# Output projection behind all token groups, in seven block products for eight

## The chip, the cores and the metric

The kernel runs on one core of one Trainium2 chip. The metric is device time in microseconds (us). Three runs of the kernel before took 2799.24, 2799.42 and 2800.96 us. All data are float32, one launch, inputs and output in the chip's memory (DRAM).

## What is computed

One layer over 2048 tokens of width 2048. An input projection to 5376 columns feeds three head groups: A (16 heads of chunked sliding-window attention over 128 keys, with sinks and a bias), B/C/X (a gated convolution of three taps), M (cross-attention into 256 memory tokens). Each output is gated, all are put side by side and mapped by one output projection, w_out (2048 x 2048):

```python
h = rmsnorm(x, ln_gain[l])
proj = h @ w_in[l]
q_a, k_a, v_a, g_a, b_c, c_c, x_c, g_c, q_m, g_m = jnp.split(proj, offsets, axis=-1)
o_a = swa_sink_attention(q_a, k_a, v_a, q_norm_a[l], k_norm_a[l], sinks[l], bias)
o_c = short_gated_conv(b_c, c_c, x_c, conv_w[l])
mem_h = rmsnorm(mem, mem_ln_gain[l])
o_m = memory_cross_attention(q_m, mem_h, w_mem_kv[l], q_norm_m[l], k_norm_m[l])
mixed = jnp.concatenate([jax.nn.silu(g_a) * o_a, jax.nn.silu(g_c) * o_c,
                         jax.nn.silu(g_m) * o_m], axis=-1)
x = x + mixed @ w_out[l]
```

## The kernel before

**Work and slots.** The tokens are four groups of 512. A float32 product is made of three matmuls on a split of each operand into a part in the type float32r and the rest: hi x hi, hi x lo, lo x hi (`split_product`, lines 1146 to 1148). Weights come in slots of 512 KB: SyncE (SP) loads a slot into `raw` (four places), ScalarE (ACT) casts its two halves to `w_hi` (`high`, line 501), GpSimd (POOL) subtracts to get `w_lo` (`low`, line 431), and TensorE (PE) runs 24 matmuls of 128x512 with it. w_hi and w_lo have room for two slots, so ACT may cast the second half of slot s+2 only when PE is through with slot s.

**A group** is 84 slots of flow and 32 of output. Slots 0 to 3 are the block KV; then come blocks of 8 slots: QM (to slot 11), QA0 (19), QA1 (27), C (35), X (43), B (51), GM (59), GC (67) and the two gates of A (75, 83). Each block fills the four PSUM banks acc0 to acc3, and the next block's first matmul into a bank waits until the bank is read. X and B are read by VectorE (DVE; lines 1030 and 1037), a gate by ACT (tanh, line 590) and DVE (line 1003, then line 1010 times the attention output). In between, at slots given by tables (`SCORES_AT` and others, in slot numbers of the group), 24 attention units run: scores on PE, softmax on DVE and ACT (lines 921 to 957), a move of the turned probabilities by DMA, the split of them (`pt_hi` on ACT, `pt_lo` on DVE, line 889), values on PE, and `attention_sum` on DVE (line 901). A unit's values come three slots after its scores; units of M start every slot, those of A nearly all every second. Every engine takes its instructions in the order in which its program lists them, so the tables set that order.

**Output part.** Behind the flow of a group stand 4 x 8 slots: for each block of 512 output columns, `mixed` (split into `mix_hi`, `mix_lo`) times w_out. In the same stretch the next group's x is prepared, one tile of 128 tokens per column block: load (line 508), squares on ACT (516), mean and scale on DVE (741 to 747), a transpose in 16 DVE operations (`x_flip`, line 775), the split into `h_hi` (ACT, 543) and `h_lo` (DVE, 784). DVE then adds x to the bank (line 1131), ACT stores.

Of the kernel before, what the change touches and what calls it, by code (L numbers as in the profile page):

```python
# [105 lines left out]
X_LOAD_S, X_SQ_S, RESID_S = 0, 2, 3  # L106
X_HIGH_AT = {5: (0, 1), 6: (2, 3)}
# [14 lines left out]
def program(nc, x, mem, ln_gain, w_in, q_norm_a, k_norm_a, sinks, conv_w, mem_ln_gain, w_mem_kv,  # L122
            q_norm_m, k_norm_m, w_out, rel_bias, one_hot, bias_rows, out):
# [3 lines left out]
    with ctx:  # L127
# [6 lines left out]
        def sem(name):  # L134
            return ctx.enter_context(nc.semaphore(name))
# [35 lines left out]
        flipped = nc.alloc_sbuf_tensor_at("flipped", [P, KT, P], F32, offset=flipped_at)  # L171
# [136 lines left out]
        def q_blocks(kind):  # L308

            return slice(12, 16) if kind == 0 else slice(4 * kind - 4, 4 * kind)  # L310

# [15 lines left out]
        def _(sp):  # L327
# [54 lines left out]
            with sp.Fori(0, GROUPS) as g:  # L382
# [22 lines left out]
                with sp.Fori(0, 4) as n:  # L405
                    for s in range(SB_SLOTS):
                        weights(s % 4, base + OUT_SLOT0 + n * SB_SLOTS + s, False,
                                w_out[256 * OUT_PAIRS[s]:256 * OUT_PAIRS[s] + 256, bass.ds(n * 512, 512)])

            end = MEM_SLOTS + GROUPS * GROUP_SLOTS  # L410
            for s in range(2):
                weights(s, end + s, False, w_out[256 * s:256 * s + 256, 0:512])
            sp.wait_ge(lo_ready, 2 * (end + 2))
# [3 lines left out]
        def _(pool):  # L417
# [43 lines left out]
            with pool.Fori(0, GROUPS) as g:  # L461
                base = g * GROUP_SLOTS + MEM_SLOTS
                for s in range(FLOW_SLOTS):
# [10 lines left out]
                with pool.Fori(0, LAST_GATES) as n:  # L474
                    for s in range(SB_SLOTS):
                        low((s + 2) % 4, base + GATE_SLOT0 + n * SB_SLOTS + s + 2)
                with pool.Fori(0, 4) as n:  # L477
                    for s in range(SB_SLOTS):
                        low((s + 2) % 4, base + OUT_SLOT0 + n * SB_SLOTS + s + 2)
                        if s == X_SQ_S:  # L480
                            x_item(g * TT + n + 2 + TT)
# [3 lines left out]
        def _(act):  # L485
# [8 lines left out]
            act.sem_inc(out_stored, 1)  # L494
# [10 lines left out]
            def x_load(i, src):  # L505
                act.wait_ge(x_turned, 8 + 4 * TT)
                act.wait_ge(x_flipped, i + 1)
                act.dma_start(xt[:, :], src).then_inc(x_in, 16)

            def x_square(tile, rows):  # L510
                if not isinstance(tile, int) or tile:
                    act.wait_ge(x_summed, tile)
                for q in range(4):
                    if not isinstance(tile, int) or tile or q:
                        act.wait_ge(x_squares, tile * 4 + q)
                    nc.scalar.activation(ps_z[:, :].rearrange("p (k c) -> p k c", c=P),  # L516
                                         rows[:, 4 * q:4 * q + 4, :], ACT.Square,
                                         accum_out=x_sq[:, q:q + 1]).then_inc(x_squares, 1)

# [17 lines left out]
            def x_high(tile, q, n):  # L537

                if q == 0:
                    act.wait_ge(x_flipped, tile - TT)  # L540
                for j in range(4):
                    k = 4 * q + j
                    hi = nc.scalar.activation(h_hi[:, k, bass.ds(n * P, P)],
                                              flipped[:, k, :],
                                              ACT.Copy, scale=gain[:, k:k + 1])
                hi.then_inc(x_hi, 1)

            def values_kv(g, slots):

                act.wait_ge(valued, g * UNITS + 1)  # L550
                act.wait_ge(x_turned, 8 + 4 * TT)
                act.wait_ge(x_flipped, g * TT + 1)
                act.wait_ge(out_stored, g * 256 + 1)
# [12 lines left out]
            def evacuate(j, name, g, slots):  # L566
# [26 lines left out]
            def gate_high(g, m, quarter):  # L593
                for b in range(4):
# [764 lines left out]
```

## Time and profile before

| | us |
|---|---|
| median of three runs | 2799.42 |
| span of the profiled execution | 2796.1 |
| PE busy | 2744.4 |
| DVE busy | 1357.8 |
| ACT busy | 1100.4 |
| POOL busy | 1420.2 |
| DMA, MB moved | 338.17 MB |

The profiled execution's own time is the span and what lies around it; the median is 3.3 us above the span. PE, DVE, ACT, POOL are the engines; PEld is PE's loading of stationary operands, which runs beside its matmuls. A row of a timeline gives start, duration, engine, line of the kernel, operation, output<-input, count, and in brackets the engine's idle time just before it and who ended it. A row of groups gives busy time and mean duration in ns. A matmul's own duration overlaps the next one; the distance of two starts is what it costs.

### The profile page before, as it was taken

What the parts mean: (1) busy time and instruction counts of PE and PEld (TensorE: products, weight loads), DVE (VectorE), ACT (ScalarE), POOL (GpSimd) and SP (SyncE); (2) the same over time, 40 slices, a digit from 0 to 9 for tenths busy, and PEclk for the clock granted to TensorE, in tenths of its full rate; (3) what the DMA queues carried; (4) which work ended last, traced back from release to release, by engine and by line L of the source; (5) the groups of instructions that cost most, each with busy time, mean ns of one, the idle gap of its engine ahead of it and who ended that gap; (6) DMA issues with size and microseconds to landing.
All of it is one profiled execution on the core that took longest, in us unless ns stands there. A gap on an engine that the chain in (4) does not pass through costs nothing.

```text
span 2796.1 us, 39537 instructions
## 1 busy us (share of the span) xinstructions
PE 2744.4 (98%) x12859; PEld 2269.3 (81%) x12859; DVE 1357.8 (49%) x2419; ACT 1100.4 (39%) x2607; POOL 1420.2 (51%) x1034
## 2 busy tenths in 40 slices
PE   6999999999999999999999999999999999999999
PEld 4888887888888888788888888788888888878887
DVE  4345575333525556614534457632534455753335
ACT  6333434434423343524432343443433334344333
POOL 5555544444455554454445555444444555445444
PEclk9999999999999999999999999999999999999999
DMA  6323333345533333334443333233453233333354
GB/s 215 118 88 105 114 102 95 106 135 169 166 96 99 105 118 98 102 98 158 159 151 98 106 98 113 85 120 112 156 182 115 87 103 113 102 98 109 128 175 140
DMA packets 215854, 338.17 MB, mean 121 GB/s; under 512 B 17702, under 2 KB 77172, under 8 KB 212852
## 3 DMA queue, kind: packets, MB, share of 16 engines
q1 hardware_dynamic: 194644, 283.49, 32.8%
q10 hardware_dynamic: 21024, 52.44, 5.6%
q8 instruction: 88, 1.44, 0.2%
q14 instruction: 98, 0.80, 0.1%
HBM read 293.13 MB, written 17.56 MB: 111 GB/s over the span
## 4 chain that ended last, share of the span: by engine, by line
issue 55%; POOL 41%; POOLq 1%; SPq 1%; DMA 1%; PE 1%; ACT 0%; DVE 0%; ACTq 0%
POOL w_lo L431 38%; POOL q_scale L438 2%; POOLq L430 1%; POOL early L446 1%; DMA raw<-in_w_mem_kv 1%; SPq L357 1%; POOL x_scale L438 0%; PE acc L1148 0%; PE acc L1146 0%; PE acc L1147 0%; ACT ps_z L516 0%; SPq L359 0%; POOLq L477 0%; ACT w_hi L501 0%; PE ps_t L1213 0%
## 5 line engine op out<-in xcount | busy, mean ns | idle before, releaser
L431 POOL TENSOR_TENSOR w_lo<-raw,w_hi 128x512 fp32r<-128x512 f32 x964 | 1313.0, 1373 | 1327.2 <-ACT w_hi L501 1324.8
L501 ACT ACTIVATE w_hi<-raw 128x512 fp32r<-128x512 f32 x964 | 592.3, 628 | 1250.9 <-PE acc L1148 1228.6
L1146 PE MATMUL acc<-h_hi,w_hi 128*128 128x512 f32 x1792 | 705.5, 394 | 0.0
L1148 PE MATMUL acc<-h_hi,w_lo 128*128 128x512 f32 x1792 | 698.9, 390 | 0.0
L1147 PE MATMUL acc<-h_lo,w_hi 128*128 128x512 f32 x1792 | 698.8, 390 | 0.0
L1146 PE MATMUL acc<-w_hi,mix_hi 128*128 128x512 f32 x1088 | 425.8, 391 | 4.0 <-POOL w_lo L431 4.0
L1147 PE MATMUL acc<-w_lo,mix_hi 128*128 128x512 f32 x1088 | 424.2, 390 | 0.0
L1148 PE MATMUL acc<-w_hi,mix_lo 128*128 128x512 f32 x1088 | 424.1, 390 | 0.0
L1146 PEld LDWEIGHTS acc<-h_hi,w_hi 128*128 128x128 f32 x1792 | 337.1, 188 | 76.0
L1148 PEld LDWEIGHTS acc<-h_hi,w_lo 128*128 128x128 f32 x1792 | 337.0, 188 | 70.8
L1147 PEld LDWEIGHTS acc<-h_lo,w_hi 128*128 128x128 f32 x1792 | 337.2, 188 | 68.5
L1146 PE MATMUL acc<-w_hi,h_hi 128*128 128x512 f32 (+1 forms) x1024 | 379.9, 371 | 0.2 <-issue 0.2
L1148 PE MATMUL acc<-w_hi,h_lo 128*128 128x512 f32 (+1 forms) x1024 | 372.1, 363 | 0.0
L1147 PE MATMUL acc<-w_lo,h_hi 128*128 128x512 f32 (+1 forms) x1024 | 371.4, 363 | 0.0
L1146 PEld LDWEIGHTS acc<-w_hi,mix_hi 128*128 128x128 f32 x1088 | 204.8, 188 | 47.7 <-issue 3.4
L1148 PEld LDWEIGHTS acc<-w_hi,mix_lo 128*128 128x128 f32 x1088 | 204.8, 188 | 42.6
L1147 PEld LDWEIGHTS acc<-w_lo,mix_hi 128*128 128x128 f32 x1088 | 204.9, 188 | 42.3
L1148 PEld LDWEIGHTS acc<-w_hi,h_lo 128*128 128x128 f32 x1024 | 193.3, 189 | 31.1
L1146 PEld LDWEIGHTS acc<-w_hi,h_hi 128*128 128x128 f32 x1024 | 193.4, 189 | 30.5 <-issue 1.2
L1147 PEld LDWEIGHTS acc<-w_lo,h_hi 128*128 128x128 f32 x1024 | 193.5, 189 | 29.5
L775 DVE STREAM_TRANSPOSE flipped<-xt 32x512 f32<-32x512 f32 x256 | 179.9, 703 | 3.8
L1003 DVE SCALAR_TENSOR_TENSOR stage<-stage,acc 128x512 f32<-128x512 f32 x64 | 43.8, 688 | 275.6 <-ACT stage L590 275.4
(150 smaller groups left out, 2264.0 us busy)
## 6 DMA issues: line engine op xcount, KB each, us to landing
raw<-in_w_in SPq DMA_DIRECT2D x336, 512.0 KB, 3.7
raw<-in_w_out SPq DMA_DIRECT2D x130, 512.0 KB, 3.6
probs_t<-blocks_t SPq DMA_DIRECT2D x384, 64.0 KB, 2.1
xt<-in_x ACTq DMA_DIRECT2D x16, 1024.0 KB, 7.6
stage<-in_x ACTq DMA_DIRECT2D x64, 256.0 KB, 4.4
out<-stage ACTq DMA_DIRECT2D x64, 256.0 KB, 3.5
raw<-in_w_mem_kv SPq DMA_DIRECT2D x16, 512.0 KB, 8.2
ungated<-in_x SPq DMA_DIRECT2D x2, 1024.0 KB, 13.8
```

The source lines that it names most:

```text
L357: sp.dma_start(first_rows(2 + tile), x[P * tile:P * tile + P, :].rearrange("p (k c) -> p k c", c=P)).then_inc(first_in[2 + tile], 16)
L430: pool.wait_ge(hi_ready, 2 * count + half + 1)
L431: nc.gpsimd.tensor_tensor(w_lo[:, at, :], raw[:, slot_mod, HALF * half:HALF * half + HALF], w_hi[:, at, :].bitcast(F32), ALU.subtract).the ...
L438: nc.gpsimd.tensor_tensor(dst, src, minus_half[:, 0:n], ALU.pow).then_inc(done, 1)
L446: nc.gpsimd.tensor_tensor(early[:, b:b + 2, :], q, q, ALU.mult).then_inc(q_squared, 1)
L501: nc.scalar.activation(w_hi[:, 2 * (slot_mod % 2) + half, :], raw[:, slot_mod, HALF * half:HALF * half + HALF], ACT.Copy).then_inc(hi_read ...
L775: last = nc.vector.transpose(flipped[32 * j:32 * j + 32, :, 32 * i:32 * i + 32], rows[32 * i:32 * i + 32, :, 32 * j:32 * j + 32])
L1003: nc.vector.scalar_tensor_tensor(out=stage[:, b, :], in0=stage[:, b, :], scalar=1.0, in1=acc[b][:, :], op0=ALU.add, op1=ALU.mult).then_inc ...
L1146: nc.tensor.matmul(dst, st[0], mv[0], start=first, stop=False)
L1147: nc.tensor.matmul(dst, st[0], mv[1], start=False, stop=False)
L1148: return nc.tensor.matmul(dst, st[1], mv[0], start=False, stop=last)
```

## The change

The output projection leaves the groups and comes once, behind all four (`OUT_SLOTS` = 112 slots for 128). Tokens are taken in two halves of 1024 (two groups of 512 each), and w_out in column halves; a pair r (of 4) is one token half with 1024 output columns, as 2x2 blocks A (512 tokens x 1024) and B (1024 x 512). The seven products of Strassen's scheme in Winograd's form (`PRODUCTS`) take the place of eight. They use sums of blocks: T1 to T4 of w_out, made once in the flow (`t_sums`, DVE, 4 operations for a 128-row strip, 4 strips a group), stored in DRAM (`w_sums`) and loaded as weights; S1 to S4 of mixed, made in the output part (`s2_tiles`, `a_sum` on DVE). The stationary operand is cast and split as it is used (`a_high` on ACT, `a_low` on DVE). Seven products accumulate in eight banks, and DVE (`combine`), ACT (a copy of the first product) and POOL (`add_resid`) join them.

Mixed rows of groups 0 to 2 are stored to DRAM from `ungated` behind each gate (`mix_store`) and loaded again at the end of group 3 and in the first products (`mixed_of`: early, h_hi's, h_lo's and ungated's room). The gates no longer split (mix_hi, mix_lo go). The next group's x is loaded, squared, scaled and transposed in the flow of groups 0 to 2 by the tables X_LOAD_AT to X_FLIP_AT, with the tiles' results in the free quarters of `early`; its split is done in slots 78 to 83 and behind. The loops over groups are written out, and the waits are on constants.

```diff
+PRODUCTS = (("A11", "B11"), ("S2", "T2"), ("A12", "B21"), ("S3", "T3"), ("S1", "T1"), ("A22", "T4"),
+            ("S4", "B22"))
+COMBINE_AT = {8: 1, 13: 2, 16: 3, 20: 4, 24: 5, 0: 6}
+X_LOAD_AT = {24: 0, 38: 1, 59: 2, 71: 3}
+X_SQUARE_AT = {27: 0, 44: 1, 61: 2, 72: 3}
+X_FLIP_AT = {29: (0, 0, 6), 31: (0, 6, 10), 35: (0, 10, 13), 37: (0, 13, 16),
+             53: (1, 0, 4), 55: (1, 4, 8), 57: (1, 8, 12), 58: (1, 12, 16),
+             64: (2, 0, 3), 65: (2, 3, 6), 66: (2, 6, 10), 67: (2, 10, 13), 70: (2, 13, 16),
+             73: (3, 0, 6), 74: (3, 6, 14), 75: (3, 14, 16)}
+T_SUM_AT = {9: 0, 28: 1, 41: 2, 54: 3}
+MIX_STORE_AT = {63: 0, 71: 1, 79: 2}
 ...
+            def x_square(g, n):
+                tile = X_TILES[n]
+                act.wait_ge(x_in, (g * TT + n) * 16 + 16)
 ...
+                nc.scalar.activation(early[:, 4 * tile:4 * tile + 4, :].rearrange("p b t -> p (b t)"),
+                                     xt[:, :], ACT.Square,
+                                     accum_out=x_sq[:, 0:1]).then_inc(x_squares, 1)
 ...
+            def t_sums(g, n):
+                done = 4 * (4 * g + n)
+                b11, b12, b21, b22 = (stage[:, c, :] for c in range(4))
+                dve.wait_ge(t_in, 16 * (4 * g + n + 1))
+                nc.vector.tensor_tensor(b11, b12, b11, ALU.subtract).then_inc(t_step, 1)
+                nc.vector.tensor_tensor(b12, b22, b12, ALU.subtract).then_inc(t_step, 1)
+                dve.wait_ge(t_step, done + 1)
+                nc.vector.tensor_tensor(b22, b22, b11, ALU.subtract).then_inc(t_step, 1)
+                dve.wait_ge(t_step, done + 3)
+                nc.vector.tensor_tensor(b21, b21, b22, ALU.subtract).then_inc(t_step, 1)
 ...
+            def tail_load(n):
+                act.wait_ge(half_used, 2 * OUT_BASE - 6 + 2 * n)
+                for k in (2 * n, HALF_K + 2 * n):
+                    mix_load(1, slice(k, k + 2))
 ...
+            def a_low(j, h):
+                dve.wait_ge(a_hi_ready, 2 * j + h + 1)
+                nc.vector.tensor_tensor(a_lo[:, 2 * (j % 2) + h, :], a_source(j, h),
+                                        a_hi[:, 2 * (j % 2) + h, :].bitcast(F32),
+                                        ALU.subtract).then_inc(a_lo_ready, 1)
+            def s2_tiles(half, k0):
+                top, low = mixed_of[2 * half], mixed_of[2 * half + 1]
+                for k in (k0, k0 + 1):
+                    nc.vector.tensor_tensor(low[:, k, :], low[:, k, :], top[:, k, :],
+                                            ALU.subtract).then_inc(s2_step, 1)
 ...
+            for j in range(OUT_SLOTS):
+                r, at = j // PAIR_SLOTS, j % PAIR_SLOTS
+                if at in COMBINE_AT and (j or at):
+                    i = COMBINE_AT[at]
+                    combine(r - (i == 6), i)
+                if j + 2 < OUT_SLOTS:
+                    for h in range(2):
+                        a_sum(j + 2, h)
+                    for h in range(2):
+                        a_low(j + 2, h)
+                if r < 2 and at < PRODUCT_SLOTS:
+                    if r == 0:
+                        dve.wait_ge(mix_in[1], 128)
+                        dve.wait_ge(mix_in[0], 64)
+                        s2_tiles(0, 2 * at)
 ...
+            def product_slot(j):
+                r, i, s = j // PAIR_SLOTS, j % PAIR_SLOTS // PRODUCT_SLOTS, j % PRODUCT_SLOTS
+                banks, par = product_banks(r, i), j % 2
+                pe.wait_ge(lo_ready, 2 * (OUT_BASE + j) + 1)
+                pe.wait_ge(a_lo_ready, 2 * j + 1)
 ...
+                        nc.tensor.matmul(banks[t][:, :], a_hi[:, at, cols], w_hi[:, at, :],
+                                         start=first, stop=False, skip_group_check=True)
```

**DVE between the softmax of slot 57 and the gate of slot 59** (first group). Before, the softmax ends in the transpose into blocks_t; the sum of an attention unit and the gate follow:

```order
L948 TENSOR_TENSOR probs<-probs,inverse 128x512
L957 STREAM_TRANSPOSE blocks_t<-probs 128x512
L901 TENSOR_TENSOR ungated<-ps_o,ungated 64x4x64 x2
L1003 SCALAR_TENSOR_TENSOR stage<-stage,acc 128x512 x4
L1009 REGISTER_ALU
L1010 SCALAR_TENSOR_TENSOR stage<-stage,ungated 128x512 x4
L1016 TENSOR_TENSOR mix_lo<-stage,mix_hi 128x512 x4
```

After, at the same place (xt is the tile of x):

```order
L1203 TENSOR_TENSOR probs<-probs,inverse 128x512
L1212 STREAM_TRANSPOSE blocks_t<-probs 128x512
L1019 STREAM_TRANSPOSE early<-xt 32x16x32 x4
L1156 TENSOR_TENSOR ungated<-ps_o,ungated 64x4x64 x2
L1019 STREAM_TRANSPOSE early<-xt 32x16x32 x4
L1258 SCALAR_TENSOR_TENSOR stage<-stage,acc 128x512 x4
L1265 SCALAR_TENSOR_TENSOR ungated<-stage,ungated 128x512 x4
```

Eight transposes of x stand ahead of the reading of the banks, and the four mix_lo are gone.

**ACT from slot 68 to the gate of slot 75**, after (w_hi are the casts of the weights, two a slot; ungated holds mixed rows). Before, only the casts stood between the two gates:

```order
L753 ACTIVATE stage<-acc 128x512 x4
L616 ACTIVATE w_hi<-raw 128x512 x2
L795 ACTIVATE ungated<-ps_o 64x4x64 x2
L616 ACTIVATE w_hi<-raw 128x512 x8
L677 DMA mixed_rows<-ungated 128x4x512
L623 DMA xt<-in_x 128x2048
L616 ACTIVATE w_hi<-raw 128x512 x2
L644 ACTIVATE early,x_sq<-xt 128x2048
L616 ACTIVATE w_hi<-raw 128x512 x4
L753 ACTIVATE stage<-acc 128x512 x4
```

A store, the load of the last tile of x (slot 71) and its squares (slot 72) have come in. On DVE the mean, the scaling and all 16 transposes of this tile stand ahead of the gate of slot 75.

**DVE at the entry into the products**, after (last gate, then the output part's first slots; mixed_51 is h_hi's room with the rows of group 1, early those of group 0):

```order
L1258 SCALAR_TENSOR_TENSOR stage<-stage,acc 128x512 x4
L1265 SCALAR_TENSOR_TENSOR ungated<-stage,ungated 128x512 x4
L1353 TENSOR_TENSOR a_lo<-early,a_hi 128x512 x2
L1361 TENSOR_TENSOR mixed_51<-mixed_51,early 128x512 x2
L1365 TENSOR_TENSOR mixed_51<-mixed_51 128x512 x2
L1353 TENSOR_TENSOR a_lo<-early,a_hi 128x512 x2
L1361 TENSOR_TENSOR mixed_51<-mixed_51,early 128x512 x2
L1365 TENSOR_TENSOR mixed_51<-mixed_51 128x512 x2
L1353 TENSOR_TENSOR a_lo<-mixed_51,a_hi 128x512 x2
```

The s2 operations on the loaded rows stand between a_lo of slot 2 and a_lo of slot 3. Before, DVE had only bank sums, one tile of x and nothing that PE's next slot waits for there.

## Rows read from the trace of the kernel before

**Rows 1.** The page: span, busy time of each engine, PE's granted clock by slice (tenths).

```profile
span 2796.1 us, 39537 instructions
...
PE 2744.4 (98%) x12859; PEld 2269.3 (81%) x12859; DVE 1357.8 (49%) x2419; ACT 1100.4 (39%) x2607; POOL 1420.2 (51%) x1034
...
PEclk9999999999999999999999999999999999999999
```

**Rows 2.** Waits of PE from 100 us on: waiting line, who ended it, total, times, longest.

```profile
PE ps_o L1265 <- DVE pt_lo L889: 10.9, 4, 2.7
...
PE ps_s L1229 <- DVE early L882: 6.4, 4, 1.6
...
PE ps_s L1237 <- ACT probs L614: 1.9, 2, 1.0
```

**Rows 3.** Timeline of PE, last output slot: start, duration, line, operation.

```profile
2787.66 0.39 PE L1146 MATMUL acc<-w_hi,mix_hi 128*128 128x512 f32 x1
...
2790.15 0.39 PE L1148 MATMUL acc<-w_hi,mix_lo 128*128 128x512 f32 x1
```

**Rows 4.** Timeline of DVE: a tile of x, mean to last transpose.

```profile
1286.02 0.16 DVE L741 TENSOR_REDUCE x_mean<-x_sq 128x1 f32<-128x4 f32 x1 [11.52 <-ACT ps_z L516]
...
1287.04 1.28 DVE L747 TENSOR_SCALAR xt<-xt,x_scale 128x2048 f32<-128x2048 f32 x1 [0.67 <-POOL x_scale L438]
...
1288.36 11.46 DVE L775 STREAM_TRANSPOSE flipped<-xt 32x512 f32<-32x512 f32 x16
```

**Rows 5.** Timeline of DVE, second group, ends of blocks X, B, GM, GC and gates.

```profile
1029.00 1.29 DVE L1030 TENSOR_TENSOR early<-acc,ungated 128x512 f32<-128x512 f32 x2
...
1076.56 2.48 DVE L1037 TENSOR_TENSOR ungated<-acc,ungated 128x512 f32<-128x512 f32 x4 [0.28 <-DVE carry L995]
...
1122.66 0.69 DVE L1003 SCALAR_TENSOR_TENSOR stage<-stage,acc 128x512 f32<-128x512 f32 x1
...
1169.76 0.65 DVE L889 TENSOR_TENSOR pt_lo<-probs_t,pt_hi 128x512 fp32r<-128x512 f32 x1
...
1174.10 0.85 DVE L901 TENSOR_TENSOR ungated<-ps_o,ungated 64x256 f32<-64x256 f32 x2 [3.69 <-ACT ungated L638]
...
1175.78 0.69 DVE L889 TENSOR_TENSOR pt_lo<-probs_t,pt_hi 128x512 fp32r<-128x512 f32 x1 [0.84 <-ACT pt_hi L622]
...
1272.02 2.48 DVE L1016 TENSOR_TENSOR mix_lo<-stage,mix_hi 128x512 f32 x4
```

**Rows 6.** Timeline of PE: first matmul of slots 44, 52, 60, 68 and 76.

```profile
1032.60 0.50 PE L1146 MATMUL acc<-h_hi,w_hi 128*128 128x512 f32 x1
...
1077.90 0.50 PE L1146 MATMUL acc<-h_hi,w_hi 128*128 128x512 f32 x1
...
1126.27 0.50 PE L1146 MATMUL acc<-h_hi,w_hi 128*128 128x512 f32 x1
...
1178.92 0.39 PE L1146 MATMUL acc<-h_hi,w_hi 128*128 128x512 f32 x1
...
1222.44 0.39 PE L1146 MATMUL acc<-h_hi,w_hi 128*128 128x512 f32 x1
```

**Rows 7.** Lines 889 and 431: duration ns min/median/max.

```profile
L889 DVE TENSOR_TENSOR pt_lo<-probs_t,pt_hi x64: 644/1254/1399, 284.7 to 2525.3; 128x512 fp32r<-128x512 f32 x64
...
L431 POOL TENSOR_TENSOR w_lo<-raw,w_hi x964: 1260/1293/3349, 13.4 to 2791.8; 128x512 fp32r<-128x512 f32 x193
```

**Rows 8.** Timeline of ACT: its cast behind slot 71.

```profile
1200.88 0.63 ACT L501 ACTIVATE w_hi<-raw 128x512 fp32r<-128x512 f32 x1 [2.09 <-PE acc L1148]
```

**Rows 9.** Groups of ACT by form: count, busy us, mean ns, idle before.

```profile
L516 ACT ACTIVATE ps_z<-xt 128x512 f32<-128x512 f32 x68 | 40.6, 597 | 4.3 <-DMA xt<-in_mem 2.7
```

**Rows 10.** Tile xt: issue of its loads (ns), time to landing (us).

```profile
L508 ACTq DMA_DIRECT2D xt<-in_x x16: 359/370/376, 598.2 to 2750.0; - x16
...
DMA to landing us min/median/max: 4.8/7.0/9.0
```

**Rows 11.** The page, DMA queues: packets, MB, share of 16 engines.

```profile
q10 hardware_dynamic: 21024, 52.44, 5.6%
```

More of the change, by code:

```diff
@@ L404, in _ @@
                     at += SB_SLOTS
[L405 to L413, printed above, removed]
+            sp.wait_ge(t_stored, 16 * 4 * GROUPS)
+            for j in range(OUT_SLOTS):
+                r, i, s = j // PAIR_SLOTS, j % PAIR_SLOTS // PRODUCT_SLOTS, j % PRODUCT_SLOTS
+                name = PRODUCTS[i][1]
+                if name in T_ROW:
+                    src = w_sums[r % 2, T_ROW[name], 256 * s:256 * s + 256, :]
+                else:
+                    row = 1024 * (name[1] == "2") + 256 * s
+                    col = 1024 * (r % 2) + 512 * (name[2] == "2")
+                    src = w_out[row:row + 256, col:col + 512]
+                weights(j % 4, OUT_BASE + j, False, src)
         @block.gpsimd
@@ L535, in mem_high, with h_high @@
                 hi.then_inc(x_hi, 1)
[L537 to L546, printed above, removed]
+            def h_high(g, k):
+                act.wait_ge(x_flipped, g * TT + TT + 1)
+                act.wait_ge(half_used, 2 * (MEM_SLOTS + (g + 1) * GROUP_SLOTS - SB_SLOTS) + k + 1)
+                nc.scalar.activation(h_hi[:, k, :].rearrange("p (t c) -> p t c", c=P),
+                                     next_rows(k), ACT.Copy,
+                                     scale=gain[:, k:k + 1]).then_inc(x_hi, 1)
@@ new lines, in _ @@
+            for g in range(GROUPS):
+                base = g * GROUP_SLOTS + MEM_SLOTS
+                last = g == GROUPS - 1
+                for s in range(GROUP_SLOTS):
+                    if last and s >= GROUP_SLOTS - 2:
+                        for h in range(2):
+                            a_low(s - GROUP_SLOTS + 2, h)
+                    if not last:
+                        if s in X_SCALE_AT:
+                            x_scale_of(g, X_SCALE_AT[s])
+                        if s in X_FLIP_AT and s >= 70:
+                            x_flip(g, *X_FLIP_AT[s])
+                        if s in H_SPLIT_AT:
+                            for k in H_SPLIT_AT[s]:
+                                h_low(g, k)
@@ L1300, in _ @@
                         last.then_inc(k_turned, 1)
-            with pe.Fori(0, GROUPS) as g:
+            for g in range(GROUPS):
                 base = g * GROUP_SLOTS + MEM_SLOTS
@@ L1322, in _ @@
                         at += 1
-                with pe.Fori(0, LAST_GATES) as n:
+                for n in range(LAST_GATES):
                     for s in range(SB_SLOTS):
```

515 lines of the change are left out of this document (378 added, 137 removed).

## The prediction

> **What bounds the kernel now.** I read the page first [rows 1]: TensorE (PE) is busy 98% of a span of 2796.1 us at full clock in every slice, VectorE (DVE) 49%, ScalarE (ACT) 39%, GpSimd (POOL) 51%. The list of waits, from 100 us on, says that PE waited some 19 us in all [rows 2]; the rest of the 52 us that PE is idle lies in the first 100 us, which the change leaves alone. So the time is the number of matmuls times their cadence. Twelve matmuls of the last slot begin between 2787.66 and 2790.15 us [rows 3]: 2.49 / 11 = 0.2265 us for one 128x512 matmul, and 24 x 0.2265 = 5.44 us for a slot. (A row's own 0.39 us overlaps its neighbour and is no cost.) The span is 3.3 us under the median of the runs; I take the difference as unchanged and count from the median.
>
> **What is removed.** Before, each of 4 groups has 4 x 8 output slots of 24 matmuls: 3072. Now there are 4 pairs x 7 products x 4 slots x 24 = 2688. The forms and the pattern of stationary operands (hi, hi, lo) are the same, so the same cadence: 384 x 0.2265 = **-87.0 us**. This is certain as far as PE stays fed. What is left to work out is where it no longer is. Both ends for every new wait follow.
>
> **What moves into the flow.** The 64 output slots of groups 0 to 2 where DVE turned the next x are gone; the 16 DVE transposes per tile (11.46 us for 16 back to back, 0.716 each) and the scaling of a tile (1.28 us) [rows 4] now stand between attention and gates of groups 0 to 2; the sums of the w_out blocks (4 DVE operations) stand there in all 4 groups. DVE has room on average. But at the end of a block PE needs its four banks back at once: the first must be read before the next block's first matmul. There DVE is in order, and what stands ahead counts. I take the second group's rows, the DVE's [rows 5] against the start of PE's next slot [rows 6], and slide the DVE by what is new. A bank is free 0.69 us after its DVE row begins.
>
> - Slot 44 (behind block X). Bank 0 is free at 1029.00 + 0.65 = 1029.7; PE wants it at 1032.60: 2.8 us of slack. In front now stand the four sums of t_sums (slot 41). Two-input SBUF work of this size takes 0.64 to 1.40 us, median 1.25 [rows 7]: 2.6 to 5.6 us for four. Waits behind each other cost less than the median each, since POOL isn't always in; I take 3.8, a stall of 1.0 us in each of 4 groups: **+4.0** (0 to 11).
> - Slot 52 (behind B). DVE works without a gap up to 1076.56, bank 0 is free at 1077.25, PE wants it at 1077.90: slack 0.65. Scale and mean of tile 0 (1.28 + 0.15) stand ahead: 0.8 us in 3 groups: **+2.4** (0 to 2.4).
> - Slot 60 (behind GM). The gate's first row begins at 1122.66, straight behind the attention of slot 58, and PE starts slot 60 at 1126.27. Eight transposes (4 at slot 57, 4 at 58) now stand ahead: 8 x 0.716 = 5.73, the gate begins at 1128.4, the bank is free at 1129.1: 2.9 us. 3 groups: 8.7. The missing mix_lo (2.5 us) lets DVE come back, and the wait of PE for probs that [rows 2] show (1.0 us, twice) goes then: **+7.7** (6 to 9).
> - Slot 68 (behind GC). From 1169.76 on DVE has pt_lo 0.65, then sits until 1174.10, sum 0.85, pt_lo at 1175.78 when its input is there, and the gate behind it. With 3 transposes before the first pt_lo, 3 behind it, 4 before the gate: 1169.76 + 2.15 + 0.65 + 2.15 = 1174.7, sum to 1175.5, pt_lo to 1176.4, four transposes to 1179.3, bank free at 1180.0; PE wants it at 1178.92. 1.1, less 0.3 won back after slot 60: 0.8 x 3 = **+2.4** (0 to 4).
> - Slot 76 (behind gate 2) is the long one, since the last tile of x is loaded only in slot 71. ACT's w_hi at 1200.88 says that slot 71 is over [rows 8]; it runs to 1201.5, one DMA issue for the mixed rows comes first (0.37 for one of this size [rows 10]), so the load of x is issued at 1201.9. An xt load of this size lands after 4.8 / 7.0 / 9.0 us (least, median, most) [rows 10]; right behind a 1 MB store I take 8. Square over 2048 columns: one of 512 takes 0.60 [rows 9], so 1.9 is an estimate that leaves out the start of three more. Mean to last transpose 13.8 us (1286.02 to 1288.36 + 11.46) [rows 4], bank 0.7, handovers 0.1. Bank free at 1201.9 + 8 + 16.5 = 1226.4; PE wants it at 1222.44: 4.0 us, in 3 groups: **+12** (2.3 with 4.8 us; 24 with 9.0 and the 3.1 us of a megabyte ahead of it, an estimate from 52.44 MB in 5.6% of the span of queue q10 [rows 11]).
>
> The Trainium skill (DMA: Bandwidth & Descriptors, the chain of events of a DMA) gives about 2.0 us plus bytes over 436 GB/s, so 4.4 us for such a tile. The trace agrees only in part: the least xt landing here is 4.8 [rows 10], the median well above; by the page's figure alone slot 76 would stall 0.4 us and the whole would be some 15 us shorter, entry included.
>
> **Entry into the products.** Product slot 3 can't start before a_low(3), which stands on DVE behind the first s2_tiles, which needs all of mixed_1. Its last pieces are asked for once the last gate is through: DVE ends the gate's second step at 1272.02 in the second group [rows 5], 6.1 us after slot 84 would begin (1222.44 + 8 x 5.44 = 1265.96); then one 1 MB load of x into stage is issued and two pieces of 0.5 MB, until +7.3. Two megabytes land at +7.3 + 4.8 + 3.1 = 15.2 at best, 7.3 + 9 + 6 = 22 at worst; I take 17.5. Then s2_tiles (four operations, 3.8) and a_low (0.8): +22.1. PE is there at 3 x 5.44 = 16.3: a stall of 5.8, and 0.7 after it since DVE has 6 such operations a slot: **+6.5** (3 to 12).
>
> **Inside the products.** ACT per slot: 4 casts of 0.63 = 2.5 of 5.44 us, finished 1.9 us after a slot's end. a_lo of the next slot but one is there 2.6 us after it, where 5.44 are allowed: 2.8 us of cover, which the bank copies and DMA waits of ACT use in part. DVE: 56 a_low, 24 a_sum, 24 bank sums a pair, 16 more in pairs 0 and 1. POOL has w_lo of 1.29 each [rows 7] (2.6 a slot) and 12 residual sums. In the slots that have s2 work, 6 DVE operations of 0.65 and 2 of POOL make 6.5 us if the two engines never overlap, 5.44 if they do: over 4 slots at most 4.3 behind, 2.8 covered. In pair 1 I take 2, in the sum slots 1 for all: **+3** (0 to 20). Queue loads: stores and loads of mixed rows, and w_sums, add some 60 MB to 338; raw is filled three slots ahead, so I put nothing for that.
>
> The Trainium skill (SBUF — State Buffer, the shared port pair) says that a DVE operation with two SBUF inputs and a GpSimd operation that reads SBUF hold a pair of ports in turn, each for its whole length. The trace agrees: pt_lo takes 0.64 when alone and up to 1.40, w_lo 1.26 to 3.35 [rows 7]. By that rule no overlap of the two is possible in the products, which is the second rival below; by the sum above part of it is.
>
> Sum: 4.0 + 2.4 + 7.7 + 2.4 + 12 + 6.5 + 3 = 38. **2799.4 - 87.0 + 38 = 2750 us.** Least and most of all terms together: 2799.4 - 87 + 11 = 2724 and 2799.4 - 87 + 82 = 2794.
>
> **Rivals.**
> 1. The waits are nearly all hidden. For it: DVE idles about half the time, loop arithmetic between its instructions goes away, and a load that lands at its least takes slot 76 and entry away. Against it: the eight transposes at slot 60 have no cover in the rows whatever lands when. Time: 7.7 + 2.3 + 3 stay: 2725.
> 2. The products are fed by DVE and POOL, not by PE: both engines take their two-input operations strictly in turn (0.65 and 1.30 each [rows 7]), so pairs 0 and 1 need 96 x 0.65 + 68 x 1.30 = 151 us of the 152 that 28 slots last, and any other wait of DVE comes on top. Each pair then loses some 6 us in its 12 sum slots and what follows the residual sums: 38 + 25 = 63, time 2775. For it: the median of pt_lo is 1.25, twice its least. Against it: four mix_lo in a row took 2.48 us [rows 5], so the two engines often miss each other.
> 3. Slower than before. The tile of slot 71 lands late: ACT's queue holds now 1 MB stores of mixed rows and w_sums, and every microsecond beyond 4 is 3 us of time. The others (26) and the gain (87) leave 61 us: 20.3 in each of 3 groups, a landing after 24.3 us. With 27 it would be 2807. Against it: 16 landings, none above 9.0 [rows 10].
>
> **Chances.** Forecast (2735 to 2764) 0.50; rival 1 0.27; rival 2 0.18; rival 3 0.05. The likeliest gives 2750. The range takes in rival 1 to its middle and rival 2 wholly: 2720 to 2779. What a measurement can tell from no change is 0.2%, 5.6 us. Faster 0.94, same 0.01, slower 0.05.
>
> **What would show it.** PE with 12475 matmuls (12859 - 384) at the same 0.2265 us and full clock; waits of PE on DVE's gate reads (banks acc) of 3 us at slot 60 and about 4 at slot 76 in groups 0 to 2, none of the two in group 3; PE at entry waiting for a_lo some 6 us, once; an idle PE of 52 + 38 = 90 us in all. Wrong is step slot 76 if xt of slot 71 lands in 5 us; wrong the step on the products if PE waits for a_lo or w_lo in them repeatedly; wrong the whole if the cadence or the clock changes.

## The result, and the profile after

The changed kernel takes **2754.3 us** (median of 4 runs, 2753.9 to 2755.2) against 2799.3 for the kernel before on the same chip: a ratio of 0.984 (95% interval 0.983 to 0.985). Forecast were 2750, in a range of 2720 to 2779.

The page of the profiled execution, against [rows 1]:

```profile
span 2752.1 us, 33713 instructions
PE 2676.1 (97%) x12475; PEld 2205.0 (80%) x12475; DVE 1680.7 (61%) x2504; ACT 1101.3 (40%) x2435; POOL 1490.3 (54%) x1042
q10 hardware_dynamic: 44496, 106.96, 11.0%
```

PE has the 384 matmuls less. The span fell by 44.0 us, though these matmuls were worth 87.0. The list of waits of PE from 100 us on (engine, tile and line waited for: us in total, times, longest), against [rows 2]:

```profile
PE acc L1482 <- DVE stage L1258: 26.1, 9, 5.1
PE ps_s L1606 <- DVE early L1137: 7.1, 4, 1.8
PE ps_s L1549 <- DVE a_lo L1353: 4.3, 3, 3.5
PE acc L1482 <- DVE early L1280: 2.6, 3, 0.9
PE acc L1482 <- POOL w_lo L532: 2.3, 4, 0.9
PE ps_s L1614 <- ACT probs L771: 2.1, 4, 1.0
PE acc L1482 <- DVE ungated L1287: 1.5, 3, 0.5
PE ps_o L1642 <- DVE pt_lo L1144: 0.9, 4, 0.3
```

acc is a bank that the flow or a product fills; L1258 is the first step of a gate, which reads the banks, L1280 and L1287 read them behind blocks X and B, L1606 and L1614 are the scores of the units of M and A, and L1614 waits here for the exp before it. With L1549's other waits (0.7) these sum to 47.6 us, where before had 19.2: +28.4. That leaves 87.0 - 28.4 - 44.0 = 14.6 us that the list of waits doesn't explain. The timeline of PE behind its two longest waits of the second group, at slots 60 and 76 (start us, duration us, ..., [idle before <- releaser]), shows where most of them went:

```profile
970.87 0.76 PE L1482 MATMUL acc<-h_hi,w_hi 128*128 128x512 f32 x1 [5.07 <-DVE stage L1258]
971.43 0.63 PE L1483 MATMUL acc<-h_lo,w_hi 128*128 128x512 f32 x1
971.86 0.63 PE L1484 MATMUL acc<-h_hi,w_lo 128*128 128x512 f32 x1
972.29 0.63 PE L1482 MATMUL acc<-h_hi,w_hi 128*128 128x512 f32 x1
...
1070.92 0.77 PE L1482 MATMUL acc<-h_hi,w_hi 128*128 128x512 f32 x1 [4.10 <-DVE stage L1258]
```

From one start to the next it is 0.43 us here, where [rows 3] had 0.2265: TensorE runs at 1.2 GHz instead of 2.4. The granted clock by windows of 25 us shows it too (window, its length, busy us of PE, PEld, DVE, ACT and POOL, then PEclk, DMA share, GB/s):

```profile
950.00:975.00 25.00, 19.93 (x91) 15.75 (x90) 20.70 (x37) 9.77 (x25) 10.40 (x8) 0.86 0.38 119
1050.00:1075.00 25.00, 20.90 (x85) 16.83 (x84) 18.60 (x26) 8.48 (x13) 10.38 (x8) 0.90 0.40 139
1075.00:1100.00 25.00, 25.00 (x108) 20.57 (x107) 8.18 (x8) 10.48 (x17) 11.05 (x9) 0.96 0.33 108
1475.00:1500.00 25.00, 21.28 (x92) 16.80 (x91) 18.43 (x34) 10.59 (x27) 10.26 (x8) 0.86 0.38 118
```

Seven waits (3.55 to 5.07 us) are followed by such a stretch. Over windows of 0.25 us from the end of each wait, (1 - granted clock) adds up to 15.6 us; before, two of its four waits for pt_lo had one, 3.4 us. So 12.2 us more are lost to the clock, and 2.4 are left. They are not short gaps: those of 0.15 us and less sum to 0.3 us behind 100 us. An estimate from the rows puts them at the edges of the waits. The list counts a wait from the end of a row of 0.39 us, though the next matmul was due 0.2265 us after that row's start, so a wait costs 0.16 us more than is listed; there are 36 waits for 11, which is 4.0 us. The other way, the stretch from the end of the last matmul to the end of the span fell from 5.6 to 3.3 us. 0.6 us stay open.

Before, one of the two waits with such a stretch ended at 459.45:

```profile
450.00:475.00 25.00, 22.26 (x99) 17.35 (x98) 16.27 (x31) 12.54 (x35) 8.63 (x7) 0.93 0.30 97
```

### The profile page after: what moved, and what is told of

Its sections match the earlier page's. It is cut to its first block, busy times and chain, and to the rows that moved or that the text cites. A ratio compares the mean times of both kernels' runs of the same rounds, so it can differ in the third digit from the quotient of the medians.

```text
span 2752.1 us, 33713 instructions
## 1 busy us (share of the span) xinstructions
PE 2676.1 (97%) x12475; PEld 2205.0 (80%) x12475; DVE 1680.7 (61%) x2504; ACT 1101.3 (40%) x2435; POOL 1490.3 (54%) x1042
## 4 chain that ended last, share of the span: by engine, by line
PE 63%; DVE 21%; ACT 4%; issue 4%; DMA 4%; SPq 2%; POOL 1%; ACTq 0%; DVEq 0%
PE acc L1482 14%; PE acc L1484 14%; PE acc L1483 14%; DVE early L1137 3%; PE acc L1549 3%; PE acc L1551 3%; PE acc L1553 3%; DVE early L1019 3%; ACT probs L771 2%; DMA probs_t<-blocks_t 2%; DVE blocks_t L1212 2%; SPq L439 1%; DVE probs L1176 1%; DVE neg_max L1188 1%; DVE probs L1203 1%
## 5 line engine op out<-in xcount | busy, mean ns | idle before, releaser
L616 ACT ACTIVATE w_hi<-raw 128x512 fp32r<-128x512 f32 x928 | 570.8, 628 | 1136.2 <-PE acc L1484 845.0
L1549 PE MATMUL acc<-w_hi,a_hi 128*128 128x512 f32 x448 | 174.8, 390 | 0.9 <-DVE a_lo L1353 0.7
L1551 PE MATMUL acc<-w_lo,a_hi 128*128 128x512 f32 x448 | 174.3, 389 | 0.0
L1553 PE MATMUL acc<-w_hi,a_lo 128*128 128x512 f32 x448 | 174.3, 389 | 0.0
L1137 DVE STREAM_TRANSPOSE early<-ungated 32x256 f32<-32x256 f32 x384 | 167.5, 436 | 5.6
L1212 DVE STREAM_TRANSPOSE blocks_t<-probs 128x512 f32<-128x512 f32 x96 | 106.4, 1109 | 77.8 <-PE ps_o L1632 75.4
L1144 DVE TENSOR_TENSOR pt_lo<-probs_t,pt_hi 128x512 fp32r<-128x512 f32 x64 | 61.5, 962 | 123.5 <-ACT pt_hi L779 123.2
L1019 DVE STREAM_TRANSPOSE early<-xt 32x512 f32<-32x512 f32 x192 | 134.5, 701 | 2.9
L1353 DVE TENSOR_TENSOR a_lo<-s_sum,a_hi 128x512 fp32r<-128x512 f32 x96 | 106.8, 1145 | 6.6 <-ACT a_hi L852 4.2
```

Of the source, the lines that this page charges most:

```text
L616: nc.scalar.activation(w_hi[:, 2 * (slot_mod % 2) + half, :], raw[:, slot_mod, HALF * half:HALF * half + HALF], ACT.Copy).then_inc(hi_read ...
L1019: last = nc.vector.transpose(flipped[32 * j:32 * j + 32, :, 32 * i:32 * i + 32], rows[32 * i:32 * i + 32, :, 32 * j:32 * j + 32])
L1137: last = nc.vector.transpose(to, rows[32 * i:32 * i + 32, :, 2 * part:2 * part + 2, 32 * j:32 * j + 32])
L1212: nc.vector.transpose(blocks_t[:, u % 2, :, :].rearrange("p j (b a) -> p j b a", b=4), probs[:, u % 2, :].rearrange("p (b c j) -> p j b c" ...
L1353: nc.vector.tensor_tensor(a_lo[:, 2 * (j % 2) + h, :], a_source(j, h), a_hi[:, 2 * (j % 2) + h, :].bitcast(F32), ALU.subtract).then_inc(a_ ...
L1549: nc.tensor.matmul(banks[t][:, :], a_hi[:, at, cols], w_hi[:, at, :], start=first, stop=False, skip_group_check=True)
```

## The experiments

**Theory:** PE waits where x's transposes and the w_out sums stand on DVE ahead of a bank read, and each longer wait is paid again, in part, by half clock behind it. **Rivals:** the clock falls on its own, whatever PE waits for; DMA traffic or the products' own work costs the time. Each experiment was compared with the kernel before on its own chip (medians 2798.1 for e1 to e4, 2799.3 for e5 to e8, 2799.1 for e9 to e11); the changed kernel ran on another, so that gains over it are good to 1 or 2 us only. Groups are counted from 0: group 1 is the second.

**1. e1_flips.** Tile 1's transposes earlier, away from slot 60:

```diff
-             53: (1, 0, 4), 55: (1, 4, 8), 57: (1, 8, 12), 58: (1, 12, 16),
+             51: (1, 0, 8), 53: (1, 8, 12), 55: (1, 12, 16),
```

> The changed kernel with the 16 DVE transposes of x tile 1 taken out of slots 53 to 58 and put at the ends of slots 51 (8), 53 (4) and 55 (4), where DVE sat idle for 5.6 us. Theory (a stall of PE at slot 60 costs its own length and is followed by a stretch at half the granted clock): the three waits at slot 60 (3.75, 5.07, 3.72 = 12.5 us) go, and with them the half-clock stretches right behind (granted clock 0.86 in 450:475, 950:975 and 1475:1500, 3.5 us each = 10.5): -22 us, 2732 us, those three windows at 1.00. Rival A (the clock falls on its own, whatever PE waits for): only the waits go, -12 us, 2742, and the clock keeps its dips. Rival B (DVE then is late for slot 60 all the same, since what was moved delays attention): under 5 us gained.

Measured: 2748.8 us (2745.6 to 2749.8), ratio 0.982 (0.981 to 0.984): 5.5 us gained by the medians, 4.3 against the kernel before on each one's chip, not 22. The waits at slot 60 and the dips behind them did go. But PE, no longer held there, came to slot 64 earlier and waited for the exp:

```profile
PE acc L1482 <- DVE stage L1258: 13.7, 6, 5.1
PE ps_s L1614 <- ACT probs L771: 9.4, 4, 2.8
```

Of 12.4 us of waits 7.3 came back, and two of the three new 2.8 us waits brought half clock of their own (slot 76 of group 2 also lost more than in the changed kernel, 2.8 us behind its wait for 1.7). Theory and rival A are both wrong in number. Rival B's (under 5) is about right, but not its reason, since no wait is left at slot 60: what the theory lacked is the next instruction that is late.

**2. e2_load.** The last tile one slot earlier (square, mean, scale and transposes too):

```diff
-X_LOAD_AT = {24: 0, 38: 1, 59: 2, 71: 3}
+X_LOAD_AT = {24: 0, 38: 1, 59: 2, 70: 3}
```

> The changed kernel with the load of the last x tile issued in slot 70 instead of 71, and its square, mean, scale and 16 transposes a slot earlier each. Theory: the waits at slot 76 (3.60, 4.10, 3.58 = 11.3 us) go, since the chain from the load's landing to the last transpose ends 5.4 us earlier, and the half-clock stretches behind them go too (7 us by the windows 550:575, 1050:1100, 1575:1600): -18 us, 2736. Rival A: waits only, -11, 2743. Rival C (the chain is bound by something else, such as ACT's order or the 1 MB store of mixed rows that is asked for in slot 71): 0 to -5.

Measured: 2735.7 us (2734.2 to 2736.0), ratio 0.978 (0.976 to 0.979): 18.6 us (17.4 on each one's chip), as expected. No wait is left at slot 76, and the windows behind it are at full clock, as in group 1:

```profile
1050.00:1075.00 25.00, 25.00 (x112) 20.72 (x111) 15.74 (x20) 9.41 (x16) 12.64 (x10) 1.00 0.32 95
```

Waits alone would have given 11.

**3. e3_tail.** `tail_load(3)` ahead of the wait for the last gate and of the load into stage:

```diff
+                if j == 0:
+                    tail_load(3)
                 if at == 0:
                     act.wait_ge(mixed, GROUPS * 16 + 1)
```

> The changed kernel with the last two loads of mixed_1 asked for ahead of the load of x into stage, so before the last gate is through (some 4 us earlier, with no megabyte in front). Theory: the wait of PE at the third product slot (3.55 us) and the stretch below full clock behind it (1.5 us) go: -5 us, 2749. Rival: DVE's order (gate, a_low, s2_tiles) sets this wait and the landing doesn't matter: 0 to -1.

Measured: 2751.3 us (2750.9 to 2753.0), ratio 0.983 (0.982 to 0.985): 3 us by the medians, within the noise of the ratios. The wait at the third product slot is 0.88 us for 3.55 and its half clock is gone; slots 60 and 76 of the second group waited 0.8 us more in this execution. So the trace, not the time, shows that the landing set this wait, as the theory said.

**4. e4_all.** The three edits together.

> The three edits together. Theory: they add up, since they are in different places of a group: -22 - 18 - 5 = -45 us, 2709 us, with PE's waits from 100 us on at about 20 us in all and full clock in every window of 25 us but the first. Rival A (clock on its own): -27, 2727.

Measured: 2724.0 us (2723.1 to 2725.1), ratio 0.973 (0.972 to 0.975): 30 us, 3 more than the three as measured (27) and 15 less than expected. What was left is in DVE's timeline ahead of slot 64 in the second group: the scaling of tile 2 stands ahead of pt_lo and the softmax.

```profile
985.07 2.31 DVE L1007 TENSOR_SCALAR xt<-xt,x_scale 128x2048 f32<-128x2048 f32 x1 [0.92 <-POOL x_scale L539]
987.30 1.78 DVE L1144 TENSOR_TENSOR pt_lo<-probs_t,pt_hi 128x512 fp32r<-128x512 f32 x1
```

**5. e5_slots.** The three edits, and more of the new DVE work in slots where DVE sat idle:

```diff
-X_LOAD_AT = {24: 0, 38: 1, 59: 2, 71: 3}
-X_SQUARE_AT = {27: 0, 44: 1, 61: 2, 72: 3}
-X_MEAN_AT = {28: 0, 45: 1, 62: 2, 72: 3}
-X_SCALE_AT = {29: 0, 46: 1, 63: 2, 73: 3}
+X_LOAD_AT = {24: 0, 38: 1, 57: 2, 70: 3}
+X_SQUARE_AT = {27: 0, 44: 1, 60: 2, 71: 3}
+X_MEAN_AT = {28: 0, 44: 1, 60: 2, 71: 3}
+X_SCALE_AT = {29: 0, 45: 1, 61: 2, 72: 3}
-             64: (2, 0, 3), 65: (2, 3, 6), 66: (2, 6, 10), 67: (2, 10, 13), 70: (2, 13, 16),
+             62: (2, 0, 5), 65: (2, 5, 9), 68: (2, 9, 16),
-T_SUM_AT = {9: 0, 28: 1, 41: 2, 54: 3}
+T_SUM_AT = {9: 0, 28: 1, 40: 2, 54: 3}
```

> The three edits before, with more of the new DVE work moved to slots in which DVE sat idle: t_sums of slot 41 at slot 40; tile 1's mean and scale one slot earlier (ahead of the turning of the queries, where the scale stood between it and slot 52's banks); tile 2 loaded in slot 57, its mean in 60 and its scale at the top of slot 61 (in the kernel with the three edits it stood at the top of slot 63 ahead of pt_lo and the softmax, and PE waited 2.8 us for the exp at slot 64 in groups 0 to 2), its transposes in slots 62, 65 and, behind the gate, 68. Theory: the wait at slot 64 falls from 2.8 to the 1.0 of group 3 (-5.4 us, and the 5.2 us of half clock behind them go), slot 52's 0.49, slot 68's 0.3 to 0.8 and most of slot 44's 0.9 go (-5): -16 from 2724, so 2708. Rival (something not looked at is late next, as at slot 64 before): not below 2718.

Measured: 2710.7 us (2709.3 to 2713.5), ratio 0.969 (0.967 to 0.971): 13 us under e4. The waits at slots 44, 48, 52, 60, 68 and 76 are gone. Slot 64's fell to 1.9 to 2.5, not to 1.0, so the theory's number was missed by 2.7; the rival's (not below 2718) is out.

**6. e6_mixlo.** Does the going of mix_lo explain that PE hardly waits for pt_lo now? In e5's kernel, behind the gate of slot 59:

```diff
+                if units == 8:
+                    for b in range(4):
+                        dve.wait_ge(gate_step, g * 4 + b + 1)
+                        nc.vector.tensor_tensor(stage[:, b, :], stage[:, b, :],
+                                                ungated[:, 4 * quarter + b, :], ALU.subtract
+                                                ).then_inc(mixed, 1)
```

> The kernel of e5_slots, with four DVE operations of two SBUF operands (128x512, 2.48 us together, results unused) put back behind the gate of slot 59, where the kernel before had its four mix_lo. Theory (the 10 us that PE no longer waits for pt_lo in this change are mix_lo's going): PE waits for pt_lo of slot 61 again, 2.7 us in each of 4 groups for 0.33 now, +9.5 us, and with half clock behind some of them (1.75 us each) up to +15. Rival (the second step of the gate had become shorter for another reason, and DVE has room there): under +3.

Measured: 2719.0 us (2718.0 to 2719.9), ratio 0.972 (0.970 to 0.973): +8.4. The waits of PE:

```profile
PE ps_o L1648 <- DVE pt_lo L1144: 10.9, 4, 2.7
PE ps_s L1620 <- ACT probs L771: 3.4, 4, 1.7
```

The 10.9 us in four waits are those of [rows 2] to the tenth. Half clock followed three of the four (+3.4 net); the later wait at slot 64 shrank by 3.8 in return.

**7. e7_no_t.** The changed kernel with no load, sum or store of w_out blocks in the flow; the products load blocks of w_out of the same size in place of the sums, so the output is another.

```diff
-T_LOAD_AT = {7: 0, 12: 1, 31: 2, 47: 3}
-T_SUM_AT = {9: 0, 28: 1, 41: 2, 54: 3}
-T_STORE_AT = {10: 0, 29: 1, 43: 2, 55: 3}
+T_LOAD_AT = {}
+T_SUM_AT = {}
+T_STORE_AT = {}
```

> The changed kernel without the sums of the w_out blocks: no load, DVE sums or store of them in the flow, and the products read w_out blocks of the same size instead, so the output is another. It gives the whole price of that part. Theory: the waits at slot 44 go (0.9 in 4 groups = 3.6), those at slot 60 shrink by the 3.8 us of t_sums in slot 54 less the 2 us of idle time that DVE had behind it (1.9 in 3 groups = 5.6), the half clock behind them stays as they are still over 1.8: -9 us, 2745. Rival (the traffic and ACT's waits for it cost as well): -15 or more.

Measured: 2748.8 us (2746.4 to 2751.2), ratio 0.982 (0.980 to 0.984): 5.5 us, less than the theory's 9 and far from the rival's 15, so the 34 MB of these loads and stores (q10 has 73.4 MB here for 107.0) are no cost that shows. Slot 60 waits 3.07 in all three groups (3.75, 5.07, 3.72 with the sums), but entry waited 5.11 for 3.55, and slot 76 of group 1 5.42 for 4.10; why is not shown. (The list names w_lo for the 3.07, but PE starts 0.15 us behind DVE's first bank read, at 965.81, as it does in the changed kernel at 970.87.)

**8. e8_no_x.** The changed kernel with a sixteenth of the x work on DVE: one transpose of 16, and 128 of 2048 columns scaled, so the output is another.

```diff
-                for ij in range(first, end):
+                for ij in range(15 if end == 16 else 16, 16):
```

> The changed kernel with nearly all of the x work on DVE left out of the flow: of each tile only the last of 16 transposes is done and 128 of 2048 columns are scaled, so the output is another; loads, squares and means stay. It gives the whole price of turning x in the flow. Theory: the waits at slots 52, 60, 68 and 76 go (1.5 + 12.5 + 2.3 + 11.3 = 27.6), and the 17.5 us lost to half clock in groups 0 to 2; at slots 61 and 64 PE waits 0.6 more each group, as in group 3 (+2): -43 us, 2711. Rival (half clock comes on its own): -26, 2728.

Measured: 2724.8 us (2720.7 to 2728.6), ratio 0.974 (0.972 to 0.976): 30 us, not 43. The rival's number (26) is nearer, but what it rests on is not: the three stretches at half clock of this trace stand behind waits of 1.86, 2.41 and 3.60 us, and those behind slots 60 and 76 are gone with their waits. Slot 64 waits 1.8 to 2.4 us (7.1 in all), and two of these waits brought half clock. The timelines show why: ACT's square of tile 2 (973.17) stands ahead of its copy of ps_o, DVE's sum waits for that, and mean and scaling wait for each other ahead of pt_lo and the softmax of slot 63:

```profile
973.17 1.90 ACT L644 ACTIVATE early<-xt 128x2048 f32<-128x2048 f32 x1
```

```profile
976.89 0.85 DVE L1156 TENSOR_TENSOR ungated<-ps_o,ungated 64x256 f32<-64x256 f32 x2 [1.36 <-ACT ungated L795]
977.77 0.15 DVE L1002 TENSOR_SCALAR x_mean<-x_sq 128x1 f32<-128x1 f32 x1
978.84 1.31 DVE L1007 TENSOR_SCALAR xt<-xt,x_scale 128x128 f32<-128x128 f32 x1 [0.92 <-POOL x_scale L539]
980.29 1.57 DVE L1144 TENSOR_TENSOR pt_lo<-probs_t,pt_hi 128x512 fp32r<-128x512 f32 x1
```

So e5, with all the work in better slots, is 14 us faster than this kernel, which has hardly any of the x work; some 4 of the 14 are e3's edit, which e5 has and this kernel has not (entry waits 3.60 here and 0.88 there, and 1.7 us at half clock behind it).

**9. and 10. e9_short, e10_long.** Dead time in e5's kernel, for waits of chosen length at slot 76. The last two transposes of x go from slot 74 to slot 75, right ahead of the gate, and multiplications of x's tile by 1.0, each waiting for the one before, stand ahead of them:

```diff
+                    for _ in range((5, 5, 7)[g]):      # e10: (10, 14, 20)
+                        nc.vector.tensor_scalar(xt[:, :], xt[:, :], 1.0, None,
+                                                ALU.mult).then_inc(gate_step, 1)
```

> The kernel of e5_slots with dead time put on DVE ahead of the gate of slot 75: the last x tile (2048 columns) is multiplied by 1.0 five times in groups 0 and 1 and seven times in group 2 (1.28 us each) before its last two transposes. The slot has 5.1, 3.8 and about 5.1 us of slack in the three groups, so PE should wait 1.5, 2.8 and 4.1 us at slot 76: +8.4 us. Theory (a wait of some 3 us or more is followed by one or two stretches of 3.4 us at half the granted clock, one under 1.8 by none, one between by either): nothing lost to the clock in group 0, 1.7 or 3.4 in group 2, either in group 1: +10 to +14 in all, 2721 to 2725. Rival (the clock falls on its own, the waits before it were a coincidence): +8.4, 2719, and dips in other places as often as here.

> The same with ten, fourteen and twenty multiplications: PE should wait about 8, 15 and 21 us at slot 76, +44 us. Theory A (what a wait costs at half clock doesn't grow with it, and part of the stretch falls into the wait itself): at most 3.4 us each, +44 to +50, 2755 to 2761. Theory B (the half-clock time grows with the length of the wait): 15 us or more on top of the 44, over 2770.

Measured: 2731.4 (2729.9 to 2733.2; ratio 0.976, 0.975 to 0.978) and 2772.5 us (2771.0 to 2773.1; ratio 0.990, 0.989 to 0.992): +20.7 and +61.9 over e5. A multiplication takes 1.23 us alone and 2.20 where POOL's w_lo runs beside it (1.53 and 1.45 on average), so the waits were longer than asked for: 3.37, 4.03, 6.83 and 11.55, 17.27, 24.17 us. Windows of e9 around the waits of 3.37 (which ended at 548.67) and 4.03 (1053.86), and of e10 behind that of 17.27 (1077.41):

```profile
525.00:550.00 25.00, 21.63 (x96) 17.62 (x95) 22.72 (x28) 8.34 (x14) 13.25 (x10) 1.00 0.38 119
550.00:575.00 25.00, 25.00 (x112) 20.69 (x111) 10.90 (x13) 10.48 (x17) 11.12 (x9) 1.00 0.42 128
1050.00:1075.00 25.00, 21.14 (x82) 17.27 (x83) 12.83 (x17) 8.86 (x15) 10.59 (x8) 0.86 0.23 64
```

```profile
1075.00:1100.00 25.00, 22.59 (x90) 18.53 (x91) 12.62 (x17) 7.99 (x13) 8.03 (x7) 0.86 0.17 45
```

The wait of 3.37 cost nothing at the clock, against the theory's "some 3 us or more". In e10 the clock was half through most of each wait, but what came behind its end was 2.6, 2.4 and 2.8 us: theory B (cost grows with length) is out; the 62 us are 53.0 of waits and 9.5 more at half clock than e5 has.

**11. e11_tune.** e5 with tile 2's scaling a slot later and no transpose before the last softmax:

```diff
-X_SCALE_AT = {29: 0, 45: 1, 61: 2, 72: 3}
+X_SCALE_AT = {29: 0, 45: 1, 62: 2, 72: 3}
-             62: (2, 0, 5), 65: (2, 5, 9), 68: (2, 9, 16),
+             65: (2, 0, 4), 66: (2, 4, 7), 68: (2, 7, 16),
```

> The kernel of e5_slots with tile 2's scaling moved from the top of slot 61 (ahead of pt_lo and the softmax, where POOL's w_lo made pt_lo 1.67 us) to the top of slot 62, and its transposes in slots 65 (4), 66 (3) and 68 (9). Theory: the wait of PE for the exp at slot 64 (1.92, 1.88, 2.45) falls to the 1.0 of group 3, -3.3 us, and with the half clock that one of them was followed by up to -5: 2706 to 2708. Rival (slot 68's banks come late again, behind seven transposes): 2709 to 2712.

Measured: **2706.1 us** (2704.9 to 2707.7), ratio 0.967 (0.966 to 0.968): the fastest kernel of the study, 93 us under the kernel before. The waits from 100 us on:

```profile
PE ps_s L1606 <- DVE early L1137: 7.1, 4, 1.8
PE ps_s L1614 <- ACT probs L771: 5.1, 4, 2.1
PE ps_s L1549 <- DVE a_lo L1353: 1.6, 3, 0.9
PE ps_o L1642 <- DVE pt_lo L1144: 1.3, 4, 0.3
PE acc L1549 <- DVE a_lo L1353: 1.3, 3, 0.5
PE acc L1482 <- DVE stage L1258: 0.2, 1, 0.2
```

16.6 us in all, under the 19.2 before, and no stretch below full clock between 75 and 2700 us. From the profiled span of before it is 92.1 us: 87.0 of matmuls, 2.6 of waits, 3.4 of clock, which leaves 0.9 over.

**The clock over all traces.** All 13 traces together, by length of a wait of PE and what (1 - granted clock) in it and behind it added up to, in us:

```
wait, us      waits   nothing   about 1.7   about 3.4   more
0.7 to 1.8      115       115           0           0      0
1.8 to 3.0       28        12          14           2      0
3.0 to 3.5        4         1           2           1      0
3.5 to 7         28         0          12          16      0
over 11           3         0           0           0      3
```

The rival that the clock falls on its own predicts no such table: no stretch below full clock between 75 and 2700 us stands apart from a wait of 1.86 us or more. Why a wait of 1.9 us had one and one of 3.37 had none stays open.

## Why the prediction was right, and where it was not

The forecast was 4.3 us low. That it came so near is in part luck: the two largest errors, 12.2 and -9.0 us, nearly cancel. By term (us):

```
term                          forecast   measured
384 matmuls less                 -87.0      -87.0
slot 44, with POOL's part         +4.0       +3.5
slot 48, w_lo                        0       +1.4
slot 52                           +2.4       +1.5
slot 60, three waits              +8.7      +12.5
relief of the pt_lo wait          -1.0      -10.0
slot 68                           +2.4       +2.3
slot 76                            +12      +11.3
entry                             +6.5       +3.6
inside the products                 +3       +1.5
slots 16 and 64                      0       +0.9
half clock behind waits              0      +12.2
edges of the waits, less the end     0       +2.4
sum                                -49      -43.9
```

(The row above the sum is what the span's -44.0 leaves; rounding makes 43.9 of it. The medians fell by 45.0.) A sign that was named missed as well: an idle PE of 90 us in all. It is 76.0 (2752.1 - 2676.1): the listed waits rose by 28.4 and not by 38, and the first 100 us and the end held 4 us less. The loss at half clock is not in it, since a slow matmul is counted as busy.

- **The cadence** held: eleven matmuls of a product start from 2600.72 to 2602.99, 0.227 each, and the count is 12475 as forecast.
- **Slot 76** was worked out rightly, step by step: the tile's load was issued at 1045.51 (+0.56), landed at 1053.40, and mean, scale (2.31 for 1.28, beside w_lo) and transposes ended at 1070.05. e2 shows that the load's slot sets it. The assumed 8 us of landing was 7.9. The Trainium skill (DMA: Bandwidth & Descriptors, the chain of events of a DMA) gives about 2.0 us plus bytes over 436 GB/s for a DMA that GpSimd issues, an estimate of 4.4 us for this size. The xt loads are issued by ACT and landed after 4.8 to 7.9 us, so the trace decides against the figure in this place.
- **Slot 60** was forecast at 2.9 and is 3.07 without the sums of w_out (e7) and 3.7 to 5.1 with them. The step that was wrong: t_sums were charged at slot 44 alone, while the group in slot 54, 3.7 us of DVE with 2.0 us of idle time behind it, stands ahead of slot 60.
- **The relief** was the forecast term that was furthest off. The prediction gave mix_lo's going 1 us, since it took two waits of 1.0 for those that end. [rows 2] showed 10.9 us in four waits for pt_lo, and their place, behind the gate and mix_lo of slot 59, would have told that they go. e6 puts them back to the tenth. In the kernel before, ahead of the first of them (PE goes on at 459.45):

```profile
456.31 2.49 DVE L1016 TENSOR_TENSOR mix_lo<-stage,mix_hi 128x512 fp32r<-128x512 f32 x4
458.72 0.68 DVE L889 TENSOR_TENSOR pt_lo<-probs_t,pt_hi 128x512 fp32r<-128x512 f32 x1
```

The waits for probs, which were to go, sum to 2.1 us where before had 1.9.
- **Half clock** was left out altogether. [rows 2] and the page's clock row in tenths gave the prediction "full clock in every slice", but before had already lost 3.4 us behind two of its 2.74 us waits, hidden by a row in which one digit stands for 90% or more of a slice of 70 us. The prediction did say that the whole would be wrong if the clock changed. The Trainium skill (TensorE: Matmul & The Clock Gate, "HAM oscillation — how this bites in real kernels") says that waits for data between groups of matmuls drop the engine to 1.2 GHz, and that this is paid at each of them. The traces agree for the long waits, with 1.5 to 3.0 us behind each of the seven of 3.55 us and more in the changed kernel; behind its 29 others, none over 1.8 us, there was nothing.
- **Entry** was oversized: the pieces of mixed_1 landed 8.6 us after their issue at 2135.8, earlier than the 10.2 taken, and no other wait follows until 2277, where 0.7 was set.
- **Rival 1** (nearly all hidden) is out: 38 us of new waits stand there. Its floor, eight transposes at slot 60 without cover, held only for the slots of the change: in e11 0.2 us of waits for gates are left. **Rival 2** (products bound by DVE and POOL) is out: PE waits 1.5 us in 609 us of products. The long durations it rested on are there (groups of DVE from 2150 to 2750 us; busy us, mean ns | idle before), but so is idle time of DVE ahead of a_lo:

```profile
L1353 DVE TENSOR_TENSOR a_lo<-s_sum,a_hi 128x512 fp32r<-128x512 f32 x96 | 106.8, 1145 | 6.6 <-ACT a_hi L852 4.2
L1353 DVE TENSOR_TENSOR a_lo<-mixed,a_hi 128x512 fp32r<-128x512 f32 x64 | 70.1, 1134 | 64.8 <-ACT a_hi L852 64.8
L1349 DVE TENSOR_TENSOR s_sum<-early,mixed 128x512 f32<-128x512 f32 x32 | 42.7, 1371 | 0.0
```

**Rival 3** is out: no xt landing over 7.9 us.

## What to carry to other kernels

When work moves onto an engine that has room on average, list for each bank hand-over what stands ahead of it in order, put the new work behind the hand-over or where that engine waits for a DMA, and then ask what PE reaches next: a wait removed (e1) lets the next one appear. In these 13 traces a wait of 3.5 to 7 us of a PE that is otherwise busy cost its length plus 1.4 to 3.1 us, one under 1.8 us its length alone, and between the two both were seen.

## What the hardware showed that was not expected

- Behind waits of 3.55 to 6.83 us in a kernel that keeps TensorE busy 97% of the time, the granted clock was at half in 28 of 28 cases, behind waits of 0.7 to 1.8 us in none of 115. Matmuls then follow each other at 0.43 us for 0.2265.
- The price doesn't grow with the wait: 2.6, 2.4 and 2.8 us behind waits of 11.6, 17.3 and 24.2 us, for 1.4 to 3.1 behind those of 3.6 to 6.8. The low stretch begins within a long wait, so a part of it falls where PE stands still anyway (1.4 us left behind the wait of 6.83).
